# Heads laid out in halves of 32 rows, queries ahead of the first branch, rotation moves of four slices

## The reference, cut to what matters

```python
def _rotate(x, ang):
    x1, x2 = jnp.split(x.astype(jnp.float32), 2, axis=-1)
    ...
    return jnp.concatenate([x1 * cos - x2 * sin, x1 * sin + x2 * cos], axis=-1)

def rope_2d(x, row, col):          # blocks one and two: 64 = 32 by row + 32 by column
    half = x.shape[-1] // 2
    xr, xc = x[..., :half], x[..., half:]
    out = jnp.concatenate([_rotate(xr, ...), _rotate(xc, ...)], axis=-1)

def chunk_gmlp(u, v, ln_g, ln_b, w_s, b_s):
    v = layernorm(v, ln_g, ln_b)
    mixed = jnp.einsum('gpq,bnqgd->bnpgd', w_s, vc) + b_s.T[None, None, :, :, None]
    return u * mixed.reshape(Bn, L, A_WIDTH)

# block one
u_a, v_a, q, k, v, gates = jnp.split(h @ w_in, ...)
y_a = chunk_gmlp(gelu(u_a), gelu(v_a), ...)
y_b = window_gqa(rope_2d(q), rope_2d(k), v, k_ctx, v_ctx, attn_sink)
```

## Time and profile before

| what | before |
|---|---|
| median of 3 runs | 3642.78 us (3639.06 to 3646.52) |
| the profiled execution | 3650.46 us, of which 3648.7 us is the span from first to last instruction |
| PE busy | 3402.3 us, 93% of the span |
| DVE busy | 1450.9 us, 40% |
| ACT busy | 702.5 us, 19% |
| DMA queue of ACT (q10) | 8.44 MB, 1.1% of 16 engines |
| DMAs at L1145 | 100, in groups of 8 (5.13 us of ACT's issue) and of 16 (11.03 us) |

### The profile page before, as it was taken

The page is one execution under the profiler, slowest core; times in us unless marked ns, Lnnn a source line. Parts: engine busy times, 40 slices in busy tenths (PEclk is TensorE's granted clock), DMA queues, the critical chain, the costliest instruction groups (busy, mean ns, idle before and its releaser), DMA issues. The chain is left out here.

```text
span 3648.7 us, 56834 instructions
## 1 busy us (share of the span) xinstructions
PE 3402.3 (93%) x24513; PEld 2416.0 (66%) x24513; DVE 1450.9 (40%) x3086; ACT 702.5 (19%) x1553; POOL 193.3 (5%) x261
## 2 busy tenths in 40 slices
PE   8989999998989888889888899999999999999988
PEld 5876888533323333257777777788888888888656
DVE  2456555210111101123655454655532646534244
ACT  2216410200000000012454115222100001101232
POOL 0000000000000000000355100300000000000000
PEclk9999999999999999999899999999999999999999
DMA  6550024599999999970000220212222322221110
GB/s 243 180 163 23 25 93 185 227 428 427 427 428 425 426 424 427 426 298 24 3 4 16 92 61 24 96 70 93 70 93 90 96 70 70 70 93 59 45 65 24
DMA packets 131128, 602.01 MB, mean 165 GB/s; under 512 B 8992, under 2 KB 39456, under 8 KB 104512
## 3 DMA queue, kind: packets, MB, share of 16 engines
q1 hardware_dynamic: 125600, 589.94, 40.8%
q10 hardware_dynamic: 5280, 8.44, 1.1%
HBM read 587.82 MB, written 2.10 MB: 162 GB/s over the span
## 5 line engine op out<-in xcount | busy, mean ns | idle before, releaser
L3070 PE MATMUL banks<-slabs,ring 128*128 128x256 f32 (+1 forms) x4456 | 1002.3, 383 | 10.6 <-POOL ring L3211 3.8
L3070 PEld LDWEIGHTS banks<-slabs,ring 128*128 128x128 f32 x4456 | 841.9, 190 | 148.0 <-issue 24.6
L2319 PE MATMUL banks<-ring,slabs 128*64 128x512 f32 x2176 | 489.3, 598 | 75.5 <-DMA ring<-in_w_exp 68.7
L2319 PEld LDWEIGHTS banks<-ring,slabs 128*64 128x64 f32 x2176 | 154.4, 137 | 390.7 <-issue 305.0
L3070 PE MATMUL banks<-ring 128*128 128x256 f32 (+1 forms) x920 | 215.1, 382 | 3.8 <-DVE ring L3211 3.1
L2490 DVE TENSOR_TENSOR work<-work,banks 128x512 f32<-128x512 f32 x32 | 22.0, 688 | 487.9 <-PE banks L2319 471.2
L393 PE MATMUL banks<-slabs,ring 128*128 128x264 f32 (+3 forms) x712 | 199.5, 437 | 4.8 <-DVE slabs L4472 1.9
L3070 PEld LDWEIGHTS banks<-ring 128*128 128x128 f32 x920 | 173.3, 190 | 32.3 <-issue 7.8
L2319 PE MATMUL banks<-slabs 128*64 128x512 f32 x768 | 171.5, 596 | 17.4 <-DMA slabs<-in_w_exp 14.5
L3418 PE MATMUL banks<-slabs,ring 128*128 128x264 f32 x768 | 172.4, 386 | 1.6 <-issue 1.6
L393 PEld LDWEIGHTS banks<-slabs,ring 128*128 128x128 f32 (+1 forms) x712 | 131.9, 189 | 62.8 <-issue 38.7
(11 more groups left out here) (635 smaller groups left out, 4372.8 us busy)
## 6 DMA issues: line engine op xcount, KB each, us to landing
ring<-in_w_exp SPq DMA_DIRECT2D x144, 2048.0 KB, 15.8
slabs<-in_w_exp SPq DMA_DIRECT2D x48, 2048.0 KB, 32.7
ring<-in_w_in SPq DMA_DIRECT2D x19, 2048.0 KB, 11.6
ring<-in_w_ff SPq DMA_DIRECT2D x16, 2048.0 KB, 8.2
ring<-in_even_w_in SPq DMA_DIRECT2D x14, 2048.0 KB, 8.5
ring<-in_w_ada SPq DMA_DIRECT2D x12, 2048.0 KB, 11.5
ring<-in_w_out SPq DMA_DIRECT2D x4, 2048.0 KB, 8.0
ring<-in_even_w_out SPq DMA_DIRECT2D x4, 2048.0 KB, 8.5
```

Source lines behind the costliest of these rows:

```text
L2319: ins = mm(out[64 * c:64 * c + CAP, :], lhsT[:, k, :], w[:, at:at + 512], start=first and k == 0, stop=last and k == 3)
L3070: last = mm(bank, a[:, k, :], b[:, k, :], start=k == 0, stop=k == h - 1)
```

## The change

Seven edits, and none of them changes how much arithmetic is done.

1. On the host, q and k columns of blocks one and two, their norm gains and the cos and sin tables are laid out with `HEAD_ORDER`: the 64 channels of a head as 0 to 15, 32 to 47, 16 to 31, 48 to 63. A partner is then 32 rows away in every rope, and `Rope` loses its argument `half`: four DMAs of 32 rows for a group, always.
2. Groups hold four slices instead of two in block one's q, in block two and in the retention, with fewer and larger scratch places. 100 DMAs at L1145 become 48.
3. DVE starts four steps behind ACT instead of two.
4. Block one makes va, then q, then u. The rotation of q no longer waits for the mixing, and its lane starts at step 20 instead of 34. Scratch of q and u is exchanged, and u's second part waits for the rotation (its place lies in u's slab).
5. `ChannelMix` starts at step 20 instead of 12, and pauses after groups 1, 3 and 5.
6. In the retention the lane starts at step 12 instead of 16, in the qb and kvb stage at 4 instead of 12, there with three steps to a slice.
7. The idle steps ahead of the exchanges of keys grow from 2 to 5 and 6.

```diff
@@ -52,0 +53,8 @@
+HEAD_ORDER = np.concatenate([np.arange(a, a + 16) for a in (0, 32, 16, 48)])
+def in_halves_of_heads(w):
+    return w.reshape(*w.shape[:-1], -1, 64)[..., HEAD_ORDER].reshape(w.shape)
@@ -55 +63 @@
-    d = np.arange(P) % 64
+    d = HEAD_ORDER[np.arange(P) % 64]
@@ -1123 +1131 @@
-    def __init__(self, core, sems, x, chunks, tokens, half, cos, sin, places, per=1, first=None, paces=None):
+    def __init__(self, core, sems, x, chunks, tokens, cos, sin, places, per=1, first=None, paces=None, lag=4):
@@ -1125 +1133 @@
-        self.half, self.cos, self.sin, self.first = half, cos, sin, first
+        self.cos, self.sin, self.first, self.lag = cos, sin, first, lag
@@ -1143,2 +1151,2 @@
-            for i in range(P // self.half):
-                rows, of = (slice(self.half * j, self.half * j + self.half) for j in (i, i ^ 1))
+            for i in range(4):
+                rows, of = (slice(32 * j, 32 * j + 32) for j in (i, i ^ 1))
@@ -1152,2 +1160,2 @@
-        yield
-        yield
+        for _ in range(self.lag):
+            yield
@@ -1157 +1165 @@
-            dve.wait_ge(moved.sem, moved.at(16 * (P // self.half) * (g // 2 + 1)))
+            dve.wait_ge(moved.sem, moved.at(64 * (g // 2 + 1)))
@@ -1504,0 +1513 @@
+    PAUSE = {1: 3, 3: 3, 5: 2}
@@ -1534,0 +1544,2 @@
+            for _ in range(self.PAUSE.get(g, 0)):
+                yield
@@ -1854 +1867 @@
-    of_va, of_u = Carve(flat[6]), Carve(flat[5])
+    of_va = Carve(flat[6])
@@ -1855,0 +1869 @@
+    few = [core.area[:, width:width + 256], core.work[:, 1792:2048], core.rstd[:, 0:256], core.rstd[:, 256:512]]
@@ -1859,3 +1873,2 @@
-        u_parts.append(products(f"u{i}", of_u, to, gelu(to)))
-    q_places = [core.area[:, width:width + 256], core.work[:, 1792:2048], core.rstd[:, 0:256], core.rstd[:, 256:512]]
-    q_parts = [products(f"q{i}", Places(*q_places), lambda p, i=i: two(q, 2 * i + p)) for i in range(2)]
+        u_parts.append(products(f"u{i}", Places(*few), to, gelu(to)))
+    q_parts = [products(f"q{i}", Carve(flat[6]), lambda p, i=i: two(q, 2 * i + p)) for i in range(2)]
@@ -1867,2 +1880,2 @@
-    places = [flat[5][:, 2048:3072]], [flat[4][:, 1536 + D * i:1536 + D * (i + 1)] for i in range(2)]
-    rope_k = Rope(core, 2, kT, 2, SEQ, 16, cos, sin, places[0], per=2)
+    places = [flat[5][:, 2048:3072]], [flat[6][:, 2048:2048 + 2 * D]]
+    rope_k = Rope(core, 2, kT, 2, SEQ, cos, sin, places[0], per=2)
@@ -1873,0 +1887 @@
+        va_parts[1].pair_done(act, 0)
@@ -1875,2 +1889,4 @@
-        act.wait_ge(core.mix["mixed_read"].sem, core.mix["mixed_read"].at(8))
-    rope_q = Rope(core, 3, q, KC, SEQ, 16, cos, sin, places[1], per=2, first=queries, paces=(4, 5, 4, 2))
+    rope_q = Rope(core, 3, q, KC, SEQ, cos, sin, places[1], per=4, first=queries, paces=(9, 5))
+    q_parts[0].place_free = lambda engine, p: va_parts[0].pair_done(engine, 0)
+    u_parts[0].place_free = lambda engine, p: q_parts[1].pair_done(engine, 1)
+    u_parts[1].place_free = lambda engine, p: engine.wait_ge(rope_q.s["step"].sem, rope_q.s["step"].at(2 * KC))
@@ -1881 +1897 @@
-    for i, part in enumerate([*va_parts, *u_parts, *q_parts, None, None]):
+    for i, part in enumerate([*va_parts, *q_parts, *u_parts, None, None]):
@@ -1891 +1907 @@
-                       lanes=[(0, [ada]), (0, [swap_c, rope_k, Idle(2), swap_k]), (12, [channel]), (34, [rope_q])])
+                       lanes=[(0, [ada]), (0, [swap_c, rope_k, Idle(5), swap_k]), (20, [channel]), (20, [rope_q])])
...
@@ -2786,2 +2802,2 @@
-    turned = Rope(core, 4, qk, 5, T, 16, core.c("grid", "cos"), core.c("grid", "sin"),
-                  [core.slab[3][:, 640 + 2 * T * i:640 + min(2 * T * (i + 1), 5 * T)] for i in range(3)], per=2)
+    turned = Rope(core, 4, qk, 5, T, core.c("grid", "cos"), core.c("grid", "sin"),
+                  [core.slab[3][:, 640:640 + 4 * T], core.slab[3][:, 640 + 4 * T:640 + 5 * T]], per=4, paces=(5, 1))
@@ -2820 +2836 @@
-    stage = SevenStage(core, [q2, *gates], banks=(0, 1, 2), lanes=[(0, [centred, outputs, normed, turned, Idle(2), other])])
+    stage = SevenStage(core, [q2, *gates], banks=(0, 1, 2), lanes=[(0, [centred, outputs, normed, turned, Idle(6), other])])
@@ -4380 +4396 @@
-    rotated = Rope(core, 2, qk, KC, SEQ, 32, cos, sin, [core.slab[3][:, 1024 * i:1024 * (i + 1)] for i in range(4)], per=2)
+    rotated = Rope(core, 2, qk, KC, SEQ, cos, sin, [core.slab[3][:, 2048 * i:2048 * (i + 1)] for i in range(2)], per=4, paces=(8, 4))
@@ -4389 +4405 @@
-               lanes=[(0, [norms]), (5, [FirstNorm(norms, lambda k: core.col("final2", k), lambda dve: qk3.plain_done(dve, 0, 3))]), (16, [rotated])]).run()
+               lanes=[(0, [norms]), (5, [FirstNorm(norms, lambda k: core.col("final2", k), lambda dve: qk3.plain_done(dve, 0, 3))]), (12, [rotated])]).run()
@@ -4443 +4459 @@
-    turn = Rope(core, 4, kr, 1, SEQ, 32, cos, sin, [core.work[:, 0:512]])
+    turn = Rope(core, 4, kr, 1, SEQ, cos, sin, [core.work[:, 0:512]])
@@ -4474,2 +4490,2 @@
-    turn = Rope(core, 0, qr, 4, SEQ, 32, cos, sin, [core.work[:, 0:512], core.work[:, 512:1024]])
-    stage = DenseStage(core, [("qb", qb_groups), ("kvb", kvb_groups)], banks=range(6), lanes=[(12, [turn])])
+    turn = Rope(core, 0, qr, 4, SEQ, cos, sin, [core.work[:, 0:512], core.work[:, 512:1024]], paces=(3, 3, 3, 1))
+    stage = DenseStage(core, [("qb", qb_groups), ("kvb", kvb_groups)], banks=range(6), lanes=[(4, [turn])])
@@ -4637 +4653 @@
-        for i, tile in enumerate([*halves("va", w_in, D), *halves("u", w_in, 0), *halves("q", w_in, 2 * D), None, None]):
+        for i, tile in enumerate([*halves("va", w_in, D), *halves("q", w_in, 2 * D), *halves("u", w_in, 0), None, None]):
...
```

More of the change, by code:

```diff
@@ L2587, in laid_out_second @@
     p2 = [x["mix_norm_g_2"], pad(mu[0]), pad(mu[1]), x["decay_w0_2"], x["icl_a0_2"], x["k_k_2"], x["k_a_2"], x["r_k_2"],
-          x["lnx_g_2"], x["lnx_b_2"], twice(x["q_norm_g_2"]), twice(x["k_norm_g_2"]), x["ffn_norm_g_2"], x["final_norm_g_2"]]
+          x["lnx_g_2"], x["lnx_b_2"], in_halves_of_heads(twice(x["q_norm_g_2"])), in_halves_of_heads(twice(x["k_norm_g_2"])), x["ffn_norm_g_2"], x["final_norm_g_2"]]
     return {
         "meta": np.ascontiguousarray(x["meta_tokens_2"].reshape(META, KC, P).transpose(2, 1, 0)),
-        "w_in_2": x["w_in_2"][0], "w_branch_rwkv": x["w_branch_rwkv_2"][0], "w_branch_attn": x["w_branch_attn_2"][0],
+        "w_in_2": np.concatenate([x["w_in_2"][0][:, :Q0], in_halves_of_heads(x["w_in_2"][0][:, Q0:K0 + P]), x["w_in_2"][0][:, K0 + P:]], 1), "w_branch_rwkv": x["w_branch_rwkv_2"][0], "w_branch_attn": x["w_branch_attn_2"][0],
         "w_out_2": x["w_out_2"][0], "w_ff1": x["w_ff1_2"][0], "w_ff2": x["w_ff2_2"][0],
@@ L4679, in laid_out @@
         "x": tokens(x["x"]), "ctx": tokens(x["ctx"]),
-        "w_ada": np.ascontiguousarray(x["w_ada"][0].reshape(KC, P, 12, SLOT_COLS).transpose(2, 1, 0, 3)).reshape(12, P, KC * SLOT_COLS), "w_in": x["w_in"][0], "w_proj_a": x["w_proj_a"][0], "w_proj_b": x["w_proj_b"][0],
+        "w_ada": np.ascontiguousarray(x["w_ada"][0].reshape(KC, P, 12, SLOT_COLS).transpose(2, 1, 0, 3)).reshape(12, P, KC * SLOT_COLS), "w_in": np.concatenate([x["w_in"][0][:, :2 * D], in_halves_of_heads(x["w_in"][0][:, 2 * D:3 * D + 256]), x["w_in"][0][:, 3 * D + 256:]], 1), "w_proj_a": x["w_proj_a"][0], "w_proj_b": x["w_proj_b"][0],
         "w_out": x["w_out"][0], "w_router": x["w_router"][0], "w_exp": expert_tiles(x),
```

## The result

The changed kernel takes 3626.19 us (median of 5 runs, 3625.37 to 3629.42); the kernel before, in the runs beside it and the three of before together, 3646.52 us (3639.06 to 3650.05). The ratio is 0.9947, with an interval of 0.9934 to 0.996: a gain of 19.3 us, between 14.6 and 24.1. The forecast was 24.8 us and 3618 us. So the time lies inside the range of 3611 to 3627 and the direction is right. It lies outside the narrower 3613 to 3622 that the prediction gives "from the bounds", and the gain of 24.8 lies just outside of what the runs allow. Another set of runs, in the experiments, gave 0.9944 (0.9931 to 0.9956), 20.4 us. One execution of the experiment x_spread took 4411.92 us at a mean granted clock of 0.746, and no ratio here uses it.

The account below looks back on a forecast made before the run. PE, busy 93% of the span, was taken to bound the kernel, so only its waits could be won: -10.7 - 1.0 - 0.4 - 0.6 - 12.1 = -24.8 us, giving 3618 us; eight-in-ten range 3611 to 3627.

Parts of the forecast that it names:

- from the bounds: Whole kernel: the forecast's own range, 3613 to 3622 us, taken from the bounds given for its terms.

Follow-up runs that it names:

- x_spread: Changed kernel with its slices of rotation set apart on DVE in block one, block two and the retention: ratio to the kernel before 0.9897, run again 0.9923.
- after: The profiled execution of the changed kernel, no further edit: 3623.6 us.
- r_after: The changed kernel once more, unchanged: ratio to the kernel before 0.9944, median 3629.83 us.
- a_lastold: Changed kernel with the qb and kvb stage in its old pace (lane from step 12, one slice a step, DVE two steps behind): ratio to before 0.9977.
- a_block1: Changed kernel with block two, retention and the last stage set back to the groups, pace and lag of before: ratio to the kernel before 0.998.

## What to carry to other kernels

Small operations of an engine that feeds the matmul engine should stand one at a time, and not in a row ahead of what the matmul engine waits for: setting eight slices apart, with their lane ahead of the mixing's, took block one's stalls from 5.9 to 1.8 us. Cost a PE stall of two to three us at its length and up to some 2 us more, for the matmuls behind it may run at half the clock. And where the forecast is a few us, take the base from the stages of two or more executions: one profiled execution can carry 3 us in a stretch that has nothing to do with the change, as four of the twelve here do. When a new order is laid out on paper, don't take the busy time of the engine that bounds the kernel as unchanged without saying so.

## What the runs showed of the hardware

- Behind the same stall of 2.69 us PE's granted clock stayed 1.00 in three executions (after, r_after, a_lastold) and fell to 0.50 in one, a_block1, which cost 1.65 us. Behind 3.48 us it was 0.50 in the one execution that had such a stall.
- Over the whole kernel the mean granted clock of a run goes with its time: 3652.1 us on average at 0.984, 3644.4 us at 0.988. Runs at 0.986 still lie between 3644.3 and 3654.6.
- Behind an idle gap of 1.3 us at the start of block one's attention the first scores ran at 2.4 GHz and the clock fell behind them in after, r_after and a_lastold; in a_block1 it was down already.
- From first issue to use a group of moves between partitions took, beside 2 MB weight tiles, 11.65 and 12.30 us as eight moves of 64 KB, 11.16 and 9.87 as four of 128 KB, and 12.28 and 13.99 as four of 256 KB. Without tiles beside them the same three landed after 6.9 to 7.0, 4.3 to 4.4 and 6.8 to 6.9 us (7.0 as four of 264 KB).
